# Branch A's normalisation and gate moved into branch B's sample part

## The chip, the cores and the metric

The kernel runs on one core of one Trainium2 chip. The metric is device time in microseconds (us) of one execution of the whole program. Three runs of the kernel before took 2506.22, 2507.71 and 2512.16 us. TensorE is called PE here, VectorE DVE, ScalarE ACT, GpSimd POOL and SyncE SP, as in the profile; ACTq and SPq are the same engines while they issue DMAs.

## The reference

One layer of a decoder is computed for a prompt of 1024 tokens and for 64 sample tokens (8 sequences of 8), 1088 columns in all. Three branches work on one normalised input:

```python
o = ((out - mean) * lax.rsqrt(var + A_GN_EPS)).reshape(B, T, A_WIDTH)   # branch A, after its delta rule
o = o * ln_w.astype(f32) + ln_b.astype(f32)
o = (o + bonus.reshape(B, T, A_WIDTH)) * g                              # g = sigmoid(lg) @ g2
...
x = x + (gates[:, :, 0] * (o_a @ w_branch_a) + gates[:, :, 1] * (o_b @ w_branch_b)
         + gates[:, :, 2] * (o_c @ w_branch_c)) @ w_out
```

Branch A is a recurrent delta rule over 6 heads of width 64, followed by the lines above: mean and variance of each head's 64 outputs, a scale, a bonus and a gate. Branch B is stick-breaking attention over 4 heads: for the prompt over its own 1024 positions, for the samples over 4096 cached positions, which lie in 32 pages of 128 rows for each sequence. Branch C is a dilated window attention. A merge and a feed-forward network follow. The output of branch A is needed only in the merge.

## The kernel before, in words

The stages run one after the other, each a block that all engines enter and leave together: load, projections (`a_project`), the delta rule (`delta`), branch A's normalisation and gate (`a_finish`), branch B's prompt part (`b_prompt`), branch B's sample part (`b_sample`), branch C, merge and feed-forward. Activations lie with channels on the 128 partitions and the 1088 tokens along the row, so branch A's 384 channels are 3 tiles ("pairs" of heads).

`delta` treats the prompt in 16 chunks of 64 tokens (lines 949 to 971) and then the 64 sample tokens (lines 978 to 1068); DVE and ACT copy the new sample states out last (`finish_state`, L779), and SP writes them to memory (L797) and waits for that (L799) before the block can end.

`a_finish` (L1198 to L1328) has the following steps. PE forms the heads' means as products with a block matrix (`put`, L1227, 9 matmuls), DVE subtracts them (L1308), ACT squares (L1278), PE sums the squares with 54 matmuls of two columns (`variance`, L1236), DVE scales (L1312), ACT takes the root (L1291) and DVE the reciprocal (L1315). PE computes the gate product (L1227, 9 more), ACT copies it out (L1283), PE spreads the factors over the partitions with 54 small matmuls (L1250), and DVE applies factor, weight with bonus, and gate (L1320, L1324, L1327). SP loads g2, the bonus and the six tiles of branch B's queries, keys and values (L1219, L1220, L1336).

`b_prompt` (L1356) turns keys and values to rows and then goes through 24 units of a 512-column block against a 128-key block. SP first issues 24 copies of cache windows from memory to memory (L1396, 8 each of 120, 504 and 2040 KB), then four outputs (L1401, L1403), then the first pages of the cache (L1412, L1414).

`b_sample` (L1571) goes through 16 chunks n, each of 4 sequences x 4 pages; it has a software pipeline written out by hand. In loop n, PE turns the keys of chunk n in four parts (`turn`, L1669; DVE copies them out, L1798), scores chunk n-1 (L1680; DVE L1804), turns back the weights of chunk n-2 (L1706; DVE L1849) and multiplies them with the values (L1719). For chunk n-1, ACT computes Abs, Exp and Ln (L1760), DVE makes from them the arguments (`arguments`: L1809, L1813, L1839, L1841), and ACT takes the exponential (L1773). Then ACT issues its share of the page loads of chunk n+2. The 32 pages (keys and values) of a chunk are shared out among the queues of SP (7 pairs), ACT (4) and POOL (5). A ring of 2 holds keys and a ring of 4 holds values: `load(n)` waits until the values of chunk n-4 are used (`pv`) and until part i of chunk n-2 has been turned (`tp`). At the end SP issues branch C's tiles (L1336, 9).

## Time and profile before

| | us |
|---|---|
| median of three runs | 2507.71 |
| the profiled execution | 2505.49 |
| its span in the profile | 2503.8 |
| `delta` ends (last copy by DVE) | at 950.4 |
| `a_finish` | 958.1 to 996.3 |
| `b_prompt` | 997.4 to 1121.5 |
| `b_sample` | 1121.7 to 1325.2 |

The times of the stages are read from the first and the last instruction of each in the timeline. PE is busy for 90% of the span, mostly in the projections and in the feed-forward network, and PEclk is the clock granted to it as a share of full speed.

### The profile page before, as it was taken

What the parts mean: (1) busy time and instruction counts of PE and PEld (TensorE: products, weight loads), DVE (VectorE), ACT (ScalarE), POOL (GpSimd) and SP (SyncE); (2) the same over time, 40 slices, a digit from 0 to 9 for tenths busy, and PEclk for the clock granted to TensorE, in tenths of its full rate; (3) what the DMA queues carried; (4) which work ended last, traced back from release to release, by engine and by line L of the source; (5) the groups of instructions that cost most, each with busy time, mean ns of one, the idle gap of its engine ahead of it and who ended that gap; (6) DMA issues with size and microseconds to landing.
All of it is one profiled execution on the core that took longest, in us unless ns stands there. A gap on an engine that the chain in (4) does not pass through costs nothing. (4 is left out here: it accounts for less than half of the span.)

```text
span 2503.8 us, 45433 instructions
## 1 busy us (share of the span) xinstructions
PE 2263.9 (90%) x19175; PEld 2062.4 (82%) x19175; DVE 1185.4 (47%) x1734; ACT 454.2 (18%) x704; POOL 666.0 (27%) x607
## 2 busy tenths in 40 slices
PE   4999999999989987777778689999999999999986
PEld 3999999999978884434446557999999999999986
DVE  2332322332123323877775444178617735762743
ACT  4000112221011112762224200130000000000012
POOL 3211111112110000554430012434324423332433
PEclk6999999999999997999898899999999999999997
DMA  6112222222210002959996164111111111111113
GB/s 164 47 47 73 79 96 79 94 81 98 86 47 4 4 5 101 323 174 335 348 357 232 63 200 162 51 34 51 34 51 43 46 39 51 43 36 49 43 47 107
DMA packets 252310, 251.92 MB, mean 101 GB/s; under 512 B 22748, under 2 KB 231365, under 8 KB 250428
## 3 DMA queue, kind: packets, MB, share of 16 engines
q1 hardware_dynamic: 213264, 177.32, 22.9%
q10 hardware_dynamic: 31484, 51.60, 6.0%
q0 software_dynamic: 7360, 20.10, 2.4%
q8 instruction: 152, 2.49, 0.4%
q14 instruction: 50, 0.41, 0.1%
HBM read 210.65 MB, written 60.13 MB: 108 GB/s over the span
## 5 line engine op out<-in xcount | busy, mean ns | idle before, releaser
L135 PE MATMUL ps<-ml,fu_wh 128*128 128x352 f32 (+1 forms) x1248 | 408.9, 328 | 7.1 <-POOL fu_wl L129 5.0
L137 PE MATMUL ps<-mh,fu_wl 128*128 128x352 f32 (+1 forms) x1248 | 408.1, 327 | 0.0
L136 PE MATMUL ps<-mh,fu_wh 128*128 128x352 f32 (+1 forms) x1248 | 407.8, 327 | 0.0
L135 PE MATMUL ps<-xl_a,ap_wh 128*128 128x352 f32 (+2 forms) x1200 | 398.4, 332 | 9.1 <-POOL ap_wl L129 9.1
L136 PE MATMUL ps<-xh_a,ap_wh 128*128 128x352 f32 (+2 forms) x1200 | 395.9, 330 | 0.0
L137 PE MATMUL ps<-xh_a,ap_wl 128*128 128x352 f32 (+2 forms) x1200 | 395.2, 329 | 0.0
L697 DVE TENSOR_TENSOR ap_raw<-ps,inv 128x384 f32<-128x384 f32 x150 | 71.2, 531 | 443.4 <-PE ps L137 443.4
L129 POOL TENSOR_TENSOR fu_wl<-fu_wt,fu_wh 128x1024 fp32r<-128x1024 f32 (+2 forms) x92 | 201.4, 2189 | 260.4 <-DVE fu_wh L124 260.4
L129 POOL TENSOR_TENSOR ap_wl<-ap_wt,ap_wh 128x1024 fp32r<-128x1024 f32 x50 | 119.9, 2398 | 513.8 <-DVE ap_wh L124 513.8
L135 PEld LDWEIGHTS ps<-ml,fu_wh 128*128 128x128 f32 x1248 | 234.8, 188 | 8.7 <-POOL fu_wl L129 5.6
L135 PEld LDWEIGHTS ps<-xl_a,ap_wh 128*128 128x128 f32 x1200 | 226.9, 189 | 15.8 <-POOL ap_wl L129 9.6
L136 PEld LDWEIGHTS ps<-mh,fu_wh 128*128 128x128 f32 x1248 | 235.5, 189 | 0.0
L137 PEld LDWEIGHTS ps<-mh,fu_wl 128*128 128x128 f32 x1248 | 234.7, 188 | 0.0
L136 PEld LDWEIGHTS ps<-xh_a,ap_wh 128*128 128x128 f32 x1200 | 226.6, 189 | 0.7 <-issue 0.7
L137 PEld LDWEIGHTS ps<-xh_a,ap_wl 128*128 128x128 f32 x1200 | 226.8, 189 | 0.0
L135 PE MATMUL ps<-fu_al,fu_wh 128*128 128x384 f32 (+1 forms) x528 | 179.3, 340 | 15.3 <-POOL fu_wl L129 10.0
L137 PE MATMUL ps<-fu_ah,fu_wl 128*128 128x384 f32 (+1 forms) x528 | 177.4, 336 | 0.0
L136 PE MATMUL ps<-fu_ah,fu_wh 128*128 128x384 f32 (+1 forms) x528 | 176.9, 335 | 0.0
L2768 DVE TENSOR_TENSOR x<-x,ps 128x352 f32<-128x352 f32 (+2 forms) x117 | 55.9, 528 | 249.5 <-PE ps L137 249.4
L2834 DVE TENSOR_TENSOR o<-ps,inv 128x384 f32<-128x384 f32 x132 | 59.6, 507 | 128.3 <-PE ps L137 128.3
L135 PEld LDWEIGHTS ps<-fu_al,fu_wh 128*128 128x128 f32 x528 | 103.0, 195 | 17.3 <-POOL fu_wl L129 11.5
L1669 PEld LDWEIGHTS ps<-cf,bs_pk 128*128 128x128 f32 x512 | 63.6, 155 | 61.5 <-DMA bs_pk<-in_cache_sb_k 50.9
(451 smaller groups left out, 3510.7 us busy)
## 6 DMA issues: line engine op xcount, KB each, us to landing
ap_wt<-in_w_in SPq DMA_DIRECT2D x50, 512.0 KB, 3.9
fu_wt<-in_w_up SPq DMA_DIRECT2D x44, 512.0 KB, 3.8
scr_pj<-ap_raw ACTq DMA_DIRECT2D x39, 544.0 KB, 2.7
bs_pk<-in_cache_sb_k SPq DMA_DIRECT2D x130, 128.0 KB, 6.7
out_win_sample<-in_cache_win SPq DMA_DIRECT2D x8, 2040.0 KB, 38.1
bs_pv<-in_cache_sb_v SPq DMA_DIRECT2D x121, 128.0 KB, 6.8
mg_gate<-scr_pj SPq DMA_DIRECT2D x24, 544.0 KB, 4.4
bs_pv<-in_cache_sb_v POOLq DMA_DIRECT2D x75, 128.0 KB, 5.8
```

What stands on the lines that cost most here:

```text
L129: return eng.tensor_tensor(dst.bitcast(F32R), x, xh, ALU.subtract)
L135: nc.tensor.matmul(out, wh, xl, start=start, stop=False)
L136: nc.tensor.matmul(out, wh, xh, start=False, stop=False)
L137: return nc.tensor.matmul(out, wl, xh, start=False, stop=stop)
L697: ins = V_.tensor_tensor(raw[:, t % 2, 1 + c0:1 + c0 + n], g.ps[:, 3 * (t % 2) + c, 0:n], g.inv[:, c0:c0 + n], ALU.mult)
L1669: mm = nc.tensor.transpose(g.ps[:, 2 * (i % 2) + p, k * P:(k + 1) * P], pk[:, n % RK, i, k, p * P:(p + 1) * P], g.ident)
L2768: ins = V_.tensor_tensor(x1[:, t, c0:c0 + m], x1[:, t, c0:c0 + m], g.ps[:, 3 * (n % 2) + c, 0:m], ALU.add)
L2834: V_.tensor_tensor(u[:, h, 2 + c0:2 + c0 + m], g.ps[:, b0 + c, 0:m], inv[:, c0:c0 + m], ALU.mult)
```

## The change

- `a_finish` is gone. Its arithmetic is done in `b_sample`, in half-loops ("slots") m = 2(n-1) and 2(n-1)+1 of loop n, in 7 parts of up to 512 columns each: MEAN in slots 0 to 6, VAR in slot 8 (54 matmuls at once), root and reciprocal up to slot 10, SPREAD in 11 to 17, GATE in 18 to 24. Each part is one small group on PE into PSUM bank 7 and one or two instructions on DVE out of it, and the two wait for each other. ACT's three squares stand after the page loads of loops 2, 3 and 4, its root with two table loads after those of loop 5. The gate product is read by DVE straight from PSUM, so ACT's copies of it are gone.
- Bank 7 becomes free because both groups of values now lie in bank 6, in its two halves.
- The sigmoid of the gate's input is computed in `a_project`; the result goes to memory in `delta` (`lgd`) and comes back in `b_prompt` (544 KB each way).
- Branch B's six tiles are loaded in `delta`, the prompt's columns once the prompt's chunks are through (`y`), the samples' columns after `z`. The sample states are written out by SP in `b_prompt`.
- In `b_prompt`, SP issues the small windows, the states, and then each larger window followed by two pages. SP's queue in `b_sample` gets g2 after the loads of n = 2 and the bonus (3 DMAs of 544 KB) after those of n = 8.

The core of the diff:

```diff
@@ delta, SP
+            eng.dma_start(g.lgd, pa[:, AT - 1, :]).then_inc(g.s_lg, 16)
...
-            for b in range(NB):
-                eng.wait_ge(x["fa"], PAIRS)
-                eng.wait_ge(x["fv"], PAIRS)
-                eng.dma_start(g.o["wkv_sample"][0, b].rearrange("h v k -> v h k"), sr[:, b]).then_inc(x["out"], 16)
+            eng.wait_ge(s["y"], 2 * (NU - 1))
+            for i in (2, 3, 4, 5, 0, 1):
+                eng.dma_start(g.qb[:, i, 0:SEQ], g.pj[i][:, 0:SEQ]).then_inc(g.s_qb[i], 16)
+            eng.wait_ge(x["z"], 1)
+            eng.dma_start(g.qb[:, :, SEQ:T], g.pj[0:6].rearrange("a p t -> p a t")[:, :, SEQ:T]).then_inc(g.s_qs, 16)
             eng.wait_ge(s["out"], 16)
-            eng.wait_ge(x["out"], 16 * NB)
+            eng.wait_ge(g.s_lg, 16)
-def a_finish(g):
...
@@ b_prompt, SP
+                for b in range(NB):
+                    window(0, b)
+                for b in range(NB):
+                    eng.dma_start(g.o["wkv_sample"][0, b].rearrange("h v k -> v h k"), g.sr[:, b]).then_inc(g.s_wkv, 16)
...
+                    window(1 + u // NB, u % NB)
+                    page(*pages[2 * u])
+                    page(*pages[2 * u + 1])
+                eng.wait_ge(g.s_wkv, 16 * NB)
+                eng.dma_start(g.oc, g.lgd).then_inc(g.s_lg, 16)
@@ b_sample
+        PARTS = [(None, SEQ, TS)] + [(p, c0, 512) for p in range(PAIRS) for c0 in (0, 512)]
+        NP = len(PARTS)
+        MEAN, VAR, SPREAD, GATE = 0, 8, 11, 11 + NP
+        slot = lambda n, late: 2 * (n - 1) + late
...
+                    if n == 2:
+                        eng.dma_start(g2, a["rwkv_g2"][0]).then_inc(f["w"], 16)
+                    if n == 8:
+                        eng.wait_ge(f["var"], 1)
+                        for p in range(PAIRS):
+                            eng.dma_start(bn[:, p, :], g.bonus[p]).then_inc(f["bn"], 16)
@@ b_sample, PE: branch_a(m), and its place in the loop
+                    elif m == VAR:
+                        eng.wait_ge(f["om"], NP)
+                        eng.wait_ge(f["sq"], PAIRS)
+                        for p in range(PAIRS):
+                            for j in range(NJ):
+                                mm = nc.tensor.matmul(sums[0:rows(j), p, j], sq[:, p, j * P:j * P + rows(j)], g.blk[:, 0:P:HD],
+                                                      start=True, stop=True)
+                        mm.then_inc(f["var"], 1)
...
                     if 1 <= n <= NN:
                         score(n - 1)
+                        branch_a(slot(n, 0))
                     if n < NN:
                         turn(n, 1)
...
                         turn(n, 2)
                         turn(n, 3)
+                    if 1 <= n < NN:
+                        branch_a(slot(n, 1))
@@ b_sample, ACT
                     load(eng, "act", n + RK)
+                    if 2 <= n < 2 + PAIRS:
+                        p = n - 2
+                        eng.wait_ge(f["om"], 2 * p + 3)
+                        nc.scalar.activation(sq[:, p, :], om[:, p, :], ACT.Square).then_inc(f["sq"], 1)
+                    if slot(n, 0) == VAR:
+                        eng.wait_ge(f["ms"], 1)
+                        nc.scalar.activation(nrm[:, :, :, :], nrm[:, :, :, :], ACT.Sqrt).then_inc(f["rt"], 1)
+                        nc.scalar.preload_act_table_set("natural_log_exp_and_others")
@@ b_sample, DVE: an early slot after turned(n, 1), a late one after arguments(n - 1)
+                        V_.tensor_tensor(dst, dst, factor, ALU.mult).then_inc(f["nx"], 1)
+                        if k and c0:
+                            eng.wait_ge(f["nx"], k + 1)
+                            eng.wait_ge(f["bn"], 16 * PAIRS)
+                            V_.scalar_tensor_tensor(out=om[:, p, :], in0=om[:, p, :], scalar=g.col("rwkv_ln_w", p),
+                                                    in1=bn[:, p, :], op0=ALU.mult, op1=ALU.add).then_inc(f["ln"], 1)
```

## Rows read from the trace of the kernel before

**Rows 1.** The page: busy time, share of the span and instructions

```profile
PE 2263.9 (90%) x19175; PEld 2062.4 (82%) x19175; DVE 1185.4 (47%) x1734; ACT 454.2 (18%) x704; POOL 666.0 (27%) x607
```

**Rows 2.** Busy time by stretch: us, engines, PEclk, DMA share, GB/s

```profile
950.50:997.40 46.90, 29.94 (x198) 21.89 (x198) 17.27 (x28) 9.54 (x15) 0.00 (x0) 0.75 0.37 128
997.40:1121.70 124.30, 95.73 (x420) 50.45 (x420) 103.50 (x137) 84.76 (x102) 65.08 (x50) 0.93 0.78 246
1144.10:1299.90 155.80, 119.13 (x1098) 75.32 (x1094) 113.45 (x136) 32.79 (x52) 65.00 (x122) 0.92 1.08 348
1179.50:1187.50 8.00, 7.30 (x79) 4.78 (x72) 5.94 (x7) 1.93 (x4) 4.42 (x9) 1.00 1.09 349
```

**Rows 3.** Timeline from delta's end to b_prompt: start, us, engine, line, work

```profile
918.70 0.64 SPq L792 DMA_DIRECT2D out_wkv_prompt<-dp_so  x1
...
949.76 0.68 DVE L779 COPY o<-ps 64x512 f32<-64x512 f32 x1 [0.19 <-PE ps L1066]
950.53 5.45 SPq L797 DMA_DIRECT2D out_wkv_sample<-o  x8
...
994.97 1.35 DVE L1327 SCALAR_TENSOR_TENSOR o<-om,par,af_gate 128x1088 f32<-128x1088 f32 x1
997.40 0.33 SPq L1389 DMA_DIRECT2D bq_later<-c_later  x1
...
1015.57 51.65 SPq L1403 DMA_DIRECT2D out_sb_k_sample<-pa  x1
```

**Rows 4.** DMA: moved in 40 slices of 1122:1325 and 1293:1318; an issue

```profile
GB/s 175 304 268 319 353 344 352 345 347 349 346 350 350 346 348 347 349 350 349 346 345 348 352 347 346 345 347 347 348 352 347 346 348 352 344 374 411 366 37 0
...
GB/s 334 359 354 352 336 341 364 346 334 356 341 338 355 359 381 381 401 415 383 415 418 390 418 425 425 383 430 397 383 418 425 411 348 306 209 139 97 42 21 0
...
pa<-scr_pj SPq DMA_DIRECT2D x6, 544.0 KB, 9.5
```

**Rows 5.** SP's waits in b_sample: total us, times, longest

```profile
SPq L1623 <- PE ps L1719: 3.2, 5, 0.9
```

**Rows 6.** Timeline of b_sample's loop 5, and two groups over 1144.1:1299.9

```profile
1179.41 0.15 DVE L1841 TENSOR_TENSOR bs_later<-bs_later,bs_l 128x1 f32<-128x1 f32 x1
1180.33 0.34 ACTq L1626 DMA_DIRECT2D bs_pk<-in_cache_sb_k  x1
1180.57 1.09 PE L1669 MATMUL ps<-cf,bs_pk 128*128 128x128 f32 x8
1184.77 1.93 PE L1719 MATMUL ps<-bs_pv,pa 128*32 128x256 f32 x32
1186.14 0.63 ACT L1760 ACTIVATE bs_l<-bs_x 128x512 f32<-128x512 f32 x1 [5.92 <-issue]
1188.13 0.69 DVE L1809 SCALAR_TENSOR_TENSOR bs_l<-bs_x,bs_l 128x512 f32<-128x512 f32 x1 [1.63 <-ACT bs_l L1760]
1189.94 0.34 SPq L1626 DMA_DIRECT2D bs_pk<-in_cache_sb_k  x1
...
L1798 DVE COPY bs_kT<-ps 128x1024 f32<-128x1024 f32 x52 | 62.9, 1220 | 31.3 <-PE ps L1680 15.6 <-PE ps L1669 15.4
L1839 DVE SCALAR_TENSOR_TENSOR bs_x<-bs_x,bs_later,bs_l 128x512 f32<-128x512 f32 x14 | 10.5, 752 | 0.5
```

**Rows 7.** Groups of instructions in a_finish: busy us, mean ns, idle before

```profile
L1227 PE MATMUL ps<-o,aux 128*128 128x352 f32 (+1 forms) x18 | 8.5, 644 | 8.5 <-PEq L782 8.5
L1236 PE MATMUL ps<-aux,af_sq 128*128 128x2 f32 (+1 forms) x54 | 6.5, 249 | 0.0
L1308 DVE SCALAR_TENSOR_TENSOR om<-ps,o 128x352 f32<-128x352 f32 (+1 forms) x9 | 4.3, 529 | 5.6 <-PE ps L1227 5.6
L1320 DVE TENSOR_TENSOR om<-om,ps 128x512 f32<-128x512 f32 (+1 forms) x9 | 4.2, 526 | 8.0 <-PE ps L1250 8.0
L1278 ACT ACTIVATE af_sq<-om 128x1088 f32<-128x1088 f32 x3 | 3.3, 1110 | 6.6 <-DVE om L1308 6.6
L1291 ACT ACT_TABLE_LOAD x1 | 1.3, 1283 | 0.0
```

More of the change, by code:

```diff
@@ L1580, in b_sample, with before @@
     NN = NG * NC
+    NJ = SEQ // P + 1
+    rows = lambda j: P if j < NJ - 1 else TS
+    PARTS = [(None, SEQ, TS)] + [(p, c0, 512) for p in range(PAIRS) for c0 in (0, 512)]
+    NP = len(PARTS)
+    MEAN, VAR, SPREAD, GATE = 0, 8, 11, 11 + NP
+    slot = lambda n, late: 2 * (n - 1) + late
+    done = lambda m, first: max(0, min(m - first, NP))
+    def before(m):
+        return done(m, MEAN), done(m, SPREAD), done(m, GATE)
     with ExitStack() as ctx:
         sb = lambda name, shape, dt=F32: ctx.enter_context(nc.sbuf_tensor(f"bs_{name}", shape, dt))
+        oa = g.oa
+        om, sq, bn = g.pa[:, 4:7, :], g.pa[:, 1:4, :], g.pa[:, 1:4, :]
+        g2 = g.pa[:, 7, 0:AW]
+        nrm = g.pa[:, 8, 0:PAIRS * NJ * 2].rearrange("t (p j h) -> t p j h", j=NJ, h=2)
+        sums = g.ps[:, 7, 0:PAIRS * NJ * 2].rearrange("t (p j h) -> t p j h", j=NJ, h=2)
         pk, pv1 = g.pk, sb("pv1", [P, RV - 1, GB, UP, 256])
@@ L1682, in score, with branch_a @@
                     mm.then_inc(s["z"], 1)
+                def branch_a(m):
+                    mean, bc, gate = before(m)
+                    if MEAN <= m < MEAN + NP:
+                        if m == MEAN:
+                            eng.wait_ge(s["zn"], 1)
+                        eng.wait_ge(f["om"], mean)
+                        put(m - MEAN, lambda p: g.blk, oa, "mean")
+                    elif m == VAR:
[6 more added lines that the diff above has]
+                        mm.then_inc(f["var"], 1)
+                    elif SPREAD <= m < SPREAD + NP:
+                        eng.wait_ge(f["rv"], 1)
+                        eng.wait_ge(f["nx"], bc)
+                        p, c0, n = PARTS[m - SPREAD]
+                        for q in range(PAIRS) if p is None else (p,):
+                            for j in (NJ - 1,) if p is None else range(c0 // P, c0 // P + 4):
+                                at = q * TS if p is None else j * P - c0
+                                for h in range(2):
+                                    mm = nc.tensor.matmul(g.ps[HD * h:HD * h + HD, 7, at:at + rows(j)],
+                                                          nrm[0:rows(j), q, j, h:h + 1].broadcast_to([rows(j), HD]),
+                                                          g.ident[0:rows(j), 0:rows(j)], start=True, stop=True)
+                        mm.then_inc(f["bc"], 1)
+                    elif GATE <= m < GATE + NP:
+                        eng.wait_ge(f["nx"], NP)
+                        eng.wait_ge(f["oa"], gate)
+                        if m == GATE:
+                            eng.wait_ge(f["w"], 16)
+                            eng.wait_ge(g.s_lg, 32)
+                        put(m - GATE, lambda p: g2[:, p * P:(p + 1) * P], None, "g")
@@ L1684, in turn_new, with put @@
+                def put(k, lhs, rhs, inc):
+                    p, c0, n = PARTS[k]
+                    for q in range(PAIRS) if p is None else (p,):
+                        at = q * TS if p is None else 0
+                        src = g.oc[:, c0:c0 + n] if rhs is None else rhs[:, q, c0:c0 + n]
+                        mm = nc.tensor.matmul(g.ps[:, 7, at:at + n], lhs(q), src, start=True, stop=True)
+                    mm.then_inc(f[inc], 1)
                 def turn_new():
```

227 lines of the change are left out of this document (80 added, 147 removed).

## The prediction

> **What bounds the kernel now.** The page's busy times come first: PE is busy for 90% of the span [rows 1], but the stages touched here are not of that kind, so they are read alone, from the table by stretch [rows 2]. Three things are to be seen in it.
>
> The 46.9 us between the last work of `delta` and the first of `b_prompt` hold only 29.94 us of PE and 17.27 us of DVE, at a clock of 0.75: a chain of short steps between engines, with nothing beside it.
>
> `b_prompt` takes 124.3 us with DVE busy for 103.5 us and the DMA engines for a share of 0.78. DVE bounds it, and the DMAs have a fifth of the time left.
>
> `b_sample` is bound by its page loads. Over 13 whole loops, from the first to the last of 14 starts of L1839 [rows 6], 155.8 us, the DMA share is over 1 at 348 GB/s, and the rate by slices is flat at 344 to 353 GB/s from the fifth slice to the 35th [rows 2, 4]. That is 155.8/13 = 11.98 us a loop. The engines have room inside it: per loop PE is busy 9.2 us and DVE 8.7 us. But a second cycle is nearly as long. From the end of DVE's arguments (1179.56) ACT takes the exponential, issues its four page pairs until 1186.1 and computes Abs, Exp and Ln until 1188.1; DVE then needs 0.69 (L1809), some 1.2 (the scan) and 0.75 (L1839) until 1190.8 [rows 6]. That is some 11.2 us. So compute can catch up some 0.8 us a loop on the DMAs, no more.
>
> **The change, part by part.**
>
> 1. The stage goes. Before, DVE's last copy ends at 949.76 + 0.68 = 950.44, SP then issues the states until 955.98 and waits for them, `a_finish` starts at 958.1, its last instruction ends at 996.32, and SP's first issue of `b_prompt` is at 997.40, 1.08 us later [rows 3]. After the change nothing is left to be waited for at the end of `delta`, so `b_prompt` starts 1.08 us after 950.44, at 951.5. Saved: 997.40 - 951.5 = 45.9 us.
>
> 2. The six tiles must be there by then. SP is free after the prompt's state went out at 918.7 [rows 3] and can issue the six about then. Before, such a tile landed 9.5 us after its issue, with 3 us to issue six [rows 4], so the last lands near 932. The samples' columns follow `z`, near 931, in 256-byte pieces: between 3 us and the whole 9.5 us of a tile, of which I take 4, so 935. Cover: 16 us. Without it the late part would stand on the path one for one. Cost 0.
>
> 3. `lgd` out of `delta` and the sigmoid in `a_project` lie beside idle engines. In `b_prompt` the DMAs get the same copies plus the states (0.8 MB) and `lgd` (0.56 MB), 1.4 MB or 4 us at 348 GB/s, into 124.3 x 0.22 = 27 us of room [rows 2]. SP's issues are now held up behind the copies in another order. Before, the queue held one output's issue for 51.65 us [rows 3] and the stage did not suffer. Bounds 0 and +15; I take 0.
>
> 4. Bytes in `b_sample`: g2 and bonus, 0.2 + 1.67 = 1.87 MB in a stage where DMA is the bound. At the page loads' 348 GB/s that is 5.4 us; at 411 GB/s, which the slices show when the tiles of branch C come in [rows 4], 4.5 us. I take 5. The four issues themselves cost SP under 2 us, and SP is not behind otherwise. The Trainium skill, page "DMA: Bandwidth & Descriptors", section "Where 436 GB/s comes from", sets about 358 GB/s as the limit of one core on the memory side. By that the bytes cost 5.2 us. The flat 348 agrees, the 381 to 425 GB/s of the tiles go beyond it, so the trace decides.
>
> 5. The MEAN slots (loops 1 to 4), and likewise GATE (10 to 13). A 512-column part costs PE 0.64 us x 512/362 = 0.9 and DVE 0.53 x 512/362 = 0.75 [rows 7]. Two of them a loop make DVE's 8.7 us 10.2 and PE's 9.2 us 11, both under 11.98. What counts is the time while ACT is busy from 1179.56 to 1188.1: 8.5 us. DVE worked 5.94 us in that stretch [rows 2], and with the two parts 7.4. It fits. The waits between PE and DVE in bank 7 may add between 0 and 1 us a loop; there are eight such loops, and I take 0 for them, since the ends of the slots fall in the gaps. Upper bound +8.
>
> 6. ACT's squares cost 1.11 us each [rows 7], right behind the page issues and ahead of Abs. ACT is in the second cycle, so loops 2 and 3 get 1.1 us longer: +2.2, before the DMAs are the bound. I count them in compute's path.
>
> 7. VAR, loop 5. This is the dear step. PE has it behind the scoring of chunk 4, where the turn of part 1 stood before, at 1180.57 [rows 6]. It waits there for the third square. But ACT does that one after its page issues, when before it began Abs, at 1186.14; so it ends at 1187.3. PE stands still for 6.7 us, and queued behind it are the turns of parts 1 to 3, the turn back and the values of chunk 3. Then come 54 matmuls, 6.5 us [rows 7], until 1193.8; the turn of part 1, 1.09; DVE's copy of it 1.22, its own VAR part 0.4, the copy of the turn back 0.7, two copies of turns 2.4 [rows 6], so L1809 starts at about 1199.6 where it started at 1188.13: +11.5 us in compute's path. The values of chunk 3, which started at 1184.77, end at about 1199.3 and not at 1186.7. All three queues wait for them before the loads of chunk 7 (a ring of 4). SP started these at 1189.94 [rows 6] and was held by such waits for only 3.2 us in the whole stage [rows 5]. Now it starts at 1199.4. All that was issued before is 11 half-chunks of 2.1 MB from 1122.5 on, 23 MB, which at the slices' rates is drained at about 1191.5. So the DMA engines stand idle for 1199.4 - 1191.5 = 8 us.
>
> 8. The root with two table loads: a root over 54 columns, under 0.3, and 2 x 1.28, together 2.8 us of ACT behind the issues of loop 5 [rows 7], in compute's path. The Trainium skill ("ScalarE: Activation LUTs", "Table sets: the hidden batching unit") prices exp followed by sqrt at two loads, some 5.3 us; by that the step would be 5.5 us. The row has 1.283 us for a load, half of the page's, and is used.
>
> 9. SPREAD, loops 7 to 9: two factors and a whole weight-and-bonus pass, 2 x 0.65 (L1320, 0.526 us for 363 columns, at 512 with the fixed part) + 1.35 (as long as L1327) = 2.7 us of DVE a loop [rows 3, 7], so 8.6 us in the 8.5 us of ACT's cover. At most 0.5 us each, 1.5 in all, in compute's path.
>
> **The sum.** Two paths run beside each other. Compute: 2.2 + 11.5 + 2.8 + 1.5 = 18, of which the eight loops after the stall give back 0.8 us each, 6.4, and the lead that the DMAs left before it, some 3: about +9. DMA: 8 idle + 5 bytes = +13. The longer one ends the stage: `b_sample` +13. Net 45.9 - 13 = 32.9 us less. The profiled execution took 2505.5 us and would take 2472.6. The median shown is 2.2 us above that execution, so the forecast is 2475 us. Its own range, with step 7 between 9 and 17 and step 5 between 0 and 4, is 2470 to 2482.
>
> **The rivals.**
>
> A. The stall is absorbed. The DMA share hardly falls at loop 5, because 7 us of landing time are in flight, and only the bytes cost: +5, so 2507.7 - 45.9 + 5 = 2467. For it: the loads are issued up to two chunks ahead. Against it: the order of issues in rows 6, where SP's loads of chunk 7 stand only 3 us behind the values that release them.
>
> B. DVE and PE become the bound in all the loops with slots. The added DVE work, 4.3 + 4.2 + 4.1 + 4.1 us and 1 us of small ones, 17.7 us in all, comes in full on top of the stall, the squares and the root, 16.5: +34, or 2496. For it: DVE and PE wait for each other twice a loop. Against it: 27% of DVE's and 24% of PE's time in this stretch is idle.
>
> C. Slower than before. Every slot of bank 7 is a meeting of PE and DVE, and each engine works off its list strictly in order. There are 22 slots. If a slot made PE wait for DVE's late part, behind the scan, and DVE for PE's, the price would be PE's 0.9, DVE's 0.75 and half of the scan and argument work, 1.5: some 3.1 us each, 68 us, and with it 2530. It decides from 45.9/22 = 2.1 us a slot. Against it: the loop's own waits are already of this kind, and much of them is slack.
>
> D. `b_prompt` is held by SP's new order. The last copies of 2040 KB are issued near its end, SP leaves the block late by some 10 us, and the sum is 2485.
>
> E. The change doesn't do what it says: the tiles land only after 951.5 because they are issued late. A full reload costs some 12 us: 2487.
>
> **How the numbers follow.** Forecast 0.45, A 0.2, B 0.2, C 0.04, D 0.06, E 0.02, the rest (a gain elsewhere) 0.03. The range takes the forecast's, A's and most of the way to B: 2463 to 2491. A measurement of this kernel can tell 0.3% from no change, 7.5 us. Only C and the far end of B or D come near that: faster 0.94, the same 0.02, slower 0.04.
>
> **What would show it.** `b_prompt` starts at 951 to 952, takes 124 us, and its first transposes don't wait for tiles. In `b_sample` PE has one gap of about 7 us ahead of a run of 54 two-column matmuls, and SP, ACT and POOL all pause their page issues there; the GB/s by slices has one hole and is flat on both sides. The stage takes 216 us. ACT has two table loads in loop 5 and none at the squares. The forecast is wrong if there is no hole (then A), if the rate is below 340 GB/s in the MEAN, SPREAD and GATE loops too (then B), or if the block before ends late by its DMAs (D).

## The result

The kernel after the change takes 2499.23 us in the median of six runs (2494.34 to 2501.34), the kernel before 2506.92 us on the same chip (2506.22 to 2512.16). The ratio is 0.9952, with a 95% interval of 0.9937 to 0.9966: 7.7 us faster by the medians, where 32.9 us were forecast. The profiled executions span 2497.9 us and, before, 2503.8 us.

The page's first rows for the kernel after answer to [rows 1]: the engines' total work is the same, as it should be, and the total says nothing about where the 46 us of the removed stage went.

```profile
span 2497.9 us, 45428 instructions
PE 2263.7 (91%) x19175; PEld 2063.4 (83%) x19175; DVE 1183.3 (47%) x1736; ACT 451.8 (18%) x696; POOL 665.7 (27%) x607
```

So the stages are timed one by one, each from the first instruction of its block to that of the next, read from the timelines (`b_prompt` from SP's load of `bq_later`, `b_sample` from POOL's clearing of `bs_qz`, branch C from SP's load of `cq_jbias`, the merge from its first matmul).

| | before | after |
|---|---|---|
| `b_prompt` starts at | 997.40 | 952.28 |
| `b_prompt` lasts | 124.4 | 126.0 |
| `b_sample` lasts | 203.5 | 238.3 |
| branch C lasts | 124.9 | 125.5 |

45.1 us are gained up to the start of `b_prompt`, 1.6 us are lost in it, and 34.8 us in `b_sample`, where 13 were forecast. Branch C and what follows it took 2.7 us more in this profile, with nothing changed in them, so that the spans differ by 5.9 us. The first gain shows in the timeline of the kernel after (start, us, engine, line, work): SP issues the six tiles at 920.24, `delta`'s last copy ends at 951.27, and `b_prompt` starts 1.01 us later. PE's first transposes then wait for the block's entry, not for a tile.

```profile
920.24 3.52 SPq L800 DMA_DIRECT2D pa<-scr_pj  x6
...
932.24 0.37 SPq L802 DMA_DIRECT2D pa<-scr_pj  x1
...
950.59 0.68 DVE L782 COPY o<-ps 64x512 f32<-64x512 f32 x1 [0.19 <-PE ps L1071]
952.28 0.33 SPq L1259 DMA_DIRECT2D bq_later<-c_later  x1
...
952.62 1.07 PE L1309 MATMUL ps<-cf,pa 128*128 128x128 f32 x8 [2.06 <-PEq L155]
```

The busy times of the two stages (columns as in [rows 2]) answer to its second row. `b_prompt` is as it was. `b_sample`'s DMA share is down to 0.87 over the stage, so the loads are no longer what fills it:

```profile
952.30:1078.00 125.70, 97.12 (x420) 50.91 (x420) 103.28 (x137) 84.72 (x102) 65.20 (x50) 0.92 0.77 254
1078.00:1316.60 238.60, 180.28 (x1596) 117.63 (x1596) 161.55 (x219) 48.67 (x75) 78.33 (x147) 0.88 0.87 285
```

The rate in 40 slices of 1078 to 1310 us, 5.8 us each, shows where. Before it was flat from the fifth slice on [rows 4]. Now there are three holes: slices 13 to 16 (1148 to 1171), slices 23 to 25 (1206 to 1223) and slices 29 and 30 (1240 to 1252); slices 18 and 19 (1177 to 1188) are a shallower dip.

```profile
GB/s 166 304 275 353 350 348 255 330 349 353 347 347 253 0 3 187 325 255 267 354 378 365 329 13 244 339 347 348 184 282 358 349 347 350 346 350 346 379 409 254
```

The lengths of the chunk loops, from one start of DVE's arguments (L1839 before, L1809 after) to the next, say the same from the compute side:

```
before  11.3 11.1 12.3 11.4 12.3 11.6 12.7 11.5 13.9 11.0 11.4 13.3 12.1 10.2
after   11.9 12.6 12.1 28.8 14.5 11.9 24.2 11.5 17.6 11.3 11.4 11.1 12.3 11.3
```

**The first long loop (28.8 us)** holds VAR. In the timeline ACT takes the third square behind its page issues, PE waits 8.55 us for it, and then the 54 matmuls take 11.46 us where [rows 7] had 6.5. DVE's copy of the next turn comes after 19.11 us of waiting, and SP, which issued its last page at 1147.78, gets to the next one at 1165.68.

```profile
1144.16 1.11 ACT L1740 ACTIVATE pa<-pa 128x1088 f32<-128x1088 f32 x1 [5.60 <-issue]
...
1145.41 11.46 PE L1611 MATMUL ps<-aux,pa 128*128 128x2 f32 x54 [8.55 <-ACT pa L1740]
...
1147.78 0.34 SPq L1534 DMA_DIRECT2D bs_pv<-in_cache_sb_v  x1
1158.81 1.23 DVE L1768 COPY bs_kT<-ps 128x1024 f32<-128x1024 f32 x1 [19.11 <-PE ps L1583]
...
1165.68 0.35 SPq L1533 DMA_DIRECT2D bs_pk<-in_cache_sb_k  x1
...
1173.54 1.28 ACT L1743 ACT_TABLE_LOAD   x1 [6.21 <-issue]
1174.84 0.25 ACT L1743 ACTIVATE pa<-pa 128x54 f32<-128x54 f32 x1
1175.10 1.28 ACT L1744 ACT_TABLE_LOAD   x1
```

Three stretches of that loop, before, in and behind the run of 54: PE is idle in the first, busy for the whole of the second at a granted clock of 0.50, that is, 1.2 GHz, and is not back at full clock in the third.

```profile
1137.80:1145.40 7.60, 0.00 (x0) 0.02 (x1) 1.90 (x4) 1.87 (x3) 2.88 (x6) 0.76 1.08 350
1145.40:1156.90 11.50, 11.49 (x55) 11.40 (x56) 0.00 (x0) 1.65 (x3) 0.00 (x0) 0.50 0.61 193
1156.90:1165.70 8.80, 8.80 (x72) 7.52 (x76) 6.30 (x9) 0.00 (x0) 0.00 (x0) 0.70 0.01 2
```

**The second (24.2 us)** is something that the prediction did not have at all. SP issues the bonus behind the pages of chunk 8 at 1191.56, and DVE's first pass with it is due 2 us later, in slot 13. It waits 13.15 us; DVE's copies of the next keys stand behind it, and so do PE's next turns and all page loads. From the first of the three issues until the wait ends the DMAs are not idle: they move 366 GB/s, 5.6 MB, of which the bonus is 1.67 MB and the rest pages issued earlier (the last row, columns as in [rows 2]).

```profile
1191.56 1.37 SPq L1547 DMA_DIRECT2D pa<-scr_bn  x3
...
1192.97 0.68 DVE L1858 TENSOR_TENSOR pa<-pa,ps 128x512 f32<-128x512 f32 x1
1206.80 1.35 DVE L1862 SCALAR_TENSOR_TENSOR pa<-pa,par 128x1088 f32<-128x1088 f32 x1 [13.15 <-DMA pa<-scr_bn]
...
1191.56:1206.80 15.24, 3.87 (x44) 2.30 (x32) 2.06 (x4) 0.63 (x1) 5.01 (x10) 0.77 1.06 366
```

**The third (17.6 us, 13.9 before)** is the loop with the first group's output. PE waits 4.67 us for DVE's copy of it, ahead of which DVE has 2 us of slot work:

```profile
1228.70 0.68 DVE L1858 TENSOR_TENSOR pa<-pa,ps 128x512 f32<-128x512 f32 x1
1229.41 1.35 DVE L1862 SCALAR_TENSOR_TENSOR pa<-pa,par 128x1088 f32<-128x1088 f32 x1
1230.68 0.41 DVE L1823 COPY bs_o<-ps 128x256 f32<-128x256 f32 x1
1231.15 0.69 PE L1686 MATMUL ps<-cf,bs_o 128*128 128x128 f32 x2 [4.67 <-DVE bs_o L1823]
```

Behind that wait PE does its next work, the turn of the output, a turn of keys and the scoring, in 5.90 us at a granted clock of 0.50; before, the same work took 4.73 us at 0.64, behind a wait of 3.61 us. So the wait costs its own length and then slower matmuls. First the row before, then after:

```profile
1239.34:1244.07 4.73, 4.73 (x26) 1.83 (x26) 0.76 (x4) 0.27 (x1) 2.93 (x6) 0.64 1.09 350
```

```profile
1231.15:1237.05 5.90, 5.90 (x27) 2.59 (x27) 0.76 (x4) 0.00 (x0) 3.12 (x6) 0.50 1.08 348
```

SP's waits for the values (total us, times, longest) sum it up. [rows 5] had 3.2 us; now it is

```profile
SPq L1530 <- PE ps L1678: 35.7, 5, 16.4
```

### The profile page after: what moved, and what is told of

It reads as the page before. It is cut to its first block and busy times, and to the rows that moved or that the text cites. A ratio compares the mean times of both kernels' runs of the same rounds, so it can differ in the third digit from the quotient of the medians.

```text
span 2497.9 us, 45428 instructions
## 1 busy us (share of the span) xinstructions
PE 2263.7 (91%) x19175; PEld 2063.4 (83%) x19175; DVE 1183.3 (47%) x1736; ACT 451.8 (18%) x696; POOL 665.7 (27%) x607
## 5 line engine op out<-in xcount | busy, mean ns | idle before, releaser
L135 PEld LDWEIGHTS ps<-xl_a,ap_wh 128*128 128x128 f32 x1200 | 226.9, 189 | 15.9 <-POOL ap_wl L129 9.7
L2862 DVE SCALAR_TENSOR_TENSOR o<-o,cw 128x1104 f32<-128x1104 f32 x44 | 109.9, 2498 | 1.6
```

The lines of the kernel that those rows point to most:

```text
L135: nc.tensor.matmul(out, wh, xl, start=start, stop=False)
L2862: V_.scalar_tensor_tensor(out=cv[:, h, 0:E], in0=u[:, h, 1:1 + E], scalar=column(g.cw[:, 1], h, j), in1=cv[:, h, 0:E], op0=ALU.mult, op1=A ...
```

## The experiments

All are variants of the changed kernel. Each was timed in five rounds beside the kernel before; the ratio is to the latter. Stage lengths and matmul times are those of each one's one profile. "The sums" are the 54 matmuls of VAR. The stage length of one profile and the median of its kernel need not agree to better than 2 or 3 us.

| | median us (range) | ratio, interval | `b_sample` | PE idle ahead of the sums | the 54 sums |
|---|---|---|---|---|---|
| the change again | 2496.97 (2494.23–2499.98) | 0.9945 [0.9932, 0.9959] | 237.2 | 8.61 | 11.47 |
| bonus early | 2486.78 (2482.14–2488.36) | 0.9903 [0.9888, 0.9917] | 226.0 | 8.34 | 11.46 |
| squares first | 2487.29 (2486.61–2488.77) | 0.9909 [0.9893, 0.9924] | 227.7 | 0.89 | 7.73 |
| both | 2479.52 (2476.07–2480.96) | 0.9871 [0.9856, 0.9886] | 218.2 | 2.62 | 10.68 |
| both, once more | 2479.91 (2474.64–2486.59) | 0.9876 [0.9857, 0.9895] | 220.4 | 2.58 | 11.24 |
| both, output first | 2476.13 (2472.56–2481.49) | 0.9870 [0.9852, 0.9889] | 213.6 | 1.17 | 8.08 |
| no arithmetic in slots | 2475.97 (2472.31–2480.32) | 0.9871 [0.9849, 0.9893] | 215.3 | | |
| also no bonus and g2 | 2471.37 (2468.22–2475.05) | 0.9845 [0.9826, 0.9865] | 207.7 | | |
| both, sums a slot later | 2481.57 (2478.25–2487.34) | 0.9890 [0.9871, 0.9909] | 219.9 | 0 | 11.33 |
| the same, 16 columns | 2483.46 (2477.58–2487.58) | 0.9886 [0.9862, 0.9909] | 220.6 | 0 | 11.47 |
| change, sums a slot later | 2488.50 (2485.04–2493.53) | 0.9920 [0.9902, 0.9938] | 227.8 | 1.42 | 11.46 |
| the same, in three slots | 2479.29 (2477.09–2481.70) | 0.9873 [0.9855, 0.9892] | 219.8 | 2.51 (third) | 2.05, 2.15, 3.85 |
| both, three slots | 2479.06 (2477.56–2483.93) | 0.9880 [0.9858, 0.9902] | 213.7 | 0 | 2.05, 2.15, 2.05 |
| and bonus by pair | 2476.96 (2470.14–2481.17) | 0.9866 [0.9844, 0.9889] | 212.9 | 0 | 2.05, 2.15, 2.05 |
| and 16 columns | 2478.19 (2472.82–2478.84) | 0.9873 [0.9852, 0.9895] | 210.8 | 0 | 2.08, 2.18, 2.08 |
| by pair, output first | 2476.75 (2473.41–2478.48) | 0.9861 [0.9842, 0.9881] | 213.7 | 0 | 2.05, 2.15, 2.05 |

**The change again.** The same kernel, on the chip of the next three, as their base.

> The changed kernel as it is, for comparison on the same chip with the next three. Both theories: 2499 us, 7 to 8 below before.

**Bonus early.** The three loads two chunks earlier in SP's list:

```diff
-                    if n == 8:
+                    if n == 6:
                         eng.wait_ge(f["var"], 1)
```

> SP issues the three bonus loads after the page loads of chunk 6 in place of chunk 8, where the trace after has SP waiting some 16 us for the values of chunk 3. Theory 1 (the gain was lost at two places, the wait for the bonus, 13.2 us, and the stall around the 54 sums of squares, 17 us): the 13.2 us of DVE's wait for scr_bn vanish, loop 7 goes from 24 us back to some 13, and the time falls by 9 to 12 us against the changed kernel, to about 2489. Theory 2 (the slots' meetings of PE and DVE cost a little in every loop, and the DMAs bound the rest): the wait is hidden by the page loads anyway, and less than 3 us comes back.

10.2 us less than the change on the same chip, and `b_sample` 11.2 less. The first hole and its 28.8 us loop stay as they were; the loop of 24.2 us is 12.0. The group row of the three passes, then that of the changed kernel (busy us, mean ns, idle ahead): the wait is gone, nothing else about the passes has changed.

```profile
L1862 DVE SCALAR_TENSOR_TENSOR pa<-pa,par 128x1088 f32<-128x1088 f32 x3 | 4.1, 1352 | 0.1
```

```profile
L1862 DVE SCALAR_TENSOR_TENSOR pa<-pa,par 128x1088 f32<-128x1088 f32 x3 | 4.1, 1351 | 13.2 <-DMA pa<-scr_bn 13.2
```

But the edit also moves the bytes. The three loads are now issued at 1156.84, in the first hole, where the DMAs stand otherwise idle, and land 3.3 to 5.6 us after their issues, for 8.1 to 14.2 before. In that stretch the DMAs move 247 GB/s, 1.69 MB, which is just the bonus:

```profile
1156.84:1163.70 6.86, 6.86 (x52) 6.26 (x56) 4.44 (x7) 0.00 (x0) 0.00 (x0) 0.62 0.70 247
```

So the 11.2 us hold two things that this run doesn't separate: the wait, and up to 4.8 us (1.67 MB at 348 GB/s) for bytes that no longer stand in the way of pages.

**Squares first.** ACT squares ahead of its page issues:

```diff
-                    load(eng, "act", n + RK)
                     if 2 <= n < 2 + PAIRS:
                         ...
+                    load(eng, "act", n + RK)
```

> ACT does each square ahead of its four page pairs, not behind them. Theory 1: PE's idle time before the sums falls from 8.6 us to about 2 to 3 us; and since the clock granted to PE was 0.5 in the 54 matmuls after that idle time, they should take 6.5 us again, not 11.5, so the loop falls from 28.8 us to some 17 and the time by 8 to 11 us against the changed kernel. If the clock has nothing to do with the idle time ahead, the matmuls stay at 11.5 us and only 5 to 6 us come back. Theory 2: 0 to 3 us.

9.7 us less. The idle time ahead of the sums falls from 8.6 to 0.89 us, and the sums need 7.73 us, not 6.5; the loop falls from 28.8 to 18.7 us. Three stretches, the second and third being the sums: the clock is 1.00 before them and in their first 4 us, and 0.56 in the rest, though PE is busy throughout.

```profile
1129.49:1137.49 8.00, 6.27 (x68) 3.20 (x66) 6.12 (x8) 2.77 (x5) 2.79 (x6) 1.00 1.09 348
...
1138.38:1142.38 4.00, 4.00 (x35) 3.95 (x36) 1.14 (x2) 0.00 (x0) 2.65 (x5) 1.00 1.08 351
1142.38:1146.11 3.73, 3.73 (x22) 3.68 (x22) 0.00 (x0) 1.89 (x3) 0.00 (x0) 0.56 1.07 346
```

**Both.**

> Both moves together. Theory 1: the two gains add up nearly fully, 16 to 22 us against the changed kernel, about 2480, and the branch B sample part takes some 218 us. Theory 2: under 5 us.

17.5 us less than the change, close to the sum of the two, 19.9: the two waits are, nearly, separate losses. `b_sample` is 218.2 us. These are near the numbers forecast for the change (216 us, 2475), but of another kernel, with a shorter wait ahead of the sums (2.62 us) than the 6.7 us of the forecast.

**No arithmetic in the slots, and then no loads either.** The first leaves out every instruction of branch A in `b_sample` on PE, DVE and ACT and keeps its loads; the second leaves out the loads too.

```diff
-                    if n == 2:
-                        eng.dma_start(g2, a["rwkv_g2"][0]).then_inc(f["w"], 16)
-                    if n == 8:
-                        for p in range(PAIRS):
-                            eng.dma_start(bn[:, p, :], g.bonus[p]).then_inc(f["bn"], 16)
```

> The changed kernel without any of branch A's arithmetic in the slots (no mean, no sums, no root, no spread, no gate on PE, DVE and ACT); all its loads stay. It gives the price of all slots together. Theory 1 as it now stands (stage before: 45 us saved; bytes some 5; the rest of the loss is in the slots, and of it the two stalls are 20): the branch B sample part takes 203.5 + 5 = 209 us, and the whole 2469. If the extra bytes are free too: 2464. If the lost time were not in the slots but in what else moved (the order of the loads, the bank that both value groups share), it would stay at 2480 or above.

> The kernel without any of branch A's arithmetic in b_sample's slots, and now also without the bonus's three loads and the gate weights' load (so branch A is neither normalised nor gated, and 1.87 MB are not read). With the loads but without the arithmetic the stage b_sample took 215.3 us against 203.5 before, its chunk loop 8 took 20.8 us with TensorE waiting 9.7 us for key pages, and the kernel 2475.97. Theory 1: those 12 us are the loads in SP's queue, between pages that the next loops need; without them b_sample takes 203 to 206 us, no loop is over 14 us, and the kernel 2464 (2461 to 2468). Theory 2: they come from the stage's place (it starts earlier against the prefetches and evictions of branch B's prompt part, or its page loads stand in another order); then b_sample stays at 212 to 216 and the time at 2473 to 2477.

The first was a miss. With no arithmetic at all the stage is still 11.8 us longer than before; its longest loop, of 20.8 us, comes behind the bonus, where PE waits for keys:

```profile
1191.06 1.97 PE L1584 MATMUL ps<-cf,bs_pk 128*128 128x128 f32 x8 [9.68 <-DMA bs_pk<-in_cache_sb_k]
```

Without the loads 7.6 of the 11.8 us are gone, and no loop exceeds 15.7 us. The kernel is 4.6 us faster by the medians and 6.5 by the ratios, whose intervals overlap. So the loads, where they stand, cost some 5 to 8 us with no arithmetic beside them; the 5 us of the forecast are not refuted. The second expectation missed too, in both its theories (2471.37 us, for 2464 or 2473 and more). The last 4.2 us against the kernel before come with the stage's new place or the profile's own spread, and stay open.

**Sums a slot later.** `VAR` from slot 8 to 9, `SPREAD` and `GATE` one further; once in the version with both edits and once in the change alone.

```diff
-    MEAN, VAR, SPREAD, GATE = 0, 8, 11, 11 + NP
+    MEAN, VAR, SPREAD, GATE = 0, 9, 12, 12 + NP
```

> Both earlier moves, and the sums of squares one slot later, behind the four turns of loop 5 instead of ahead of three of them; spread and gate one slot later as well. Theory 1: the 54 matmuls no longer stand ahead of the turns that DVE waits for, so the loop of 21.8 us becomes some 15 to 17 and the time falls by another 4 to 7 us against the kernel with both moves, to about 2474. Rival (PE's own work is what the loop is short of, wherever it stands): under 2 us.

> The changed kernel with nothing but the sums one slot later (bonus and squares as changed). It tells how much of the stall is the wait for the third square and how much the order on PE. Theory 1: by the time of the late slot the square is done, PE does not stand still before the sums and stays at full clock, so it gains as much as moving the squares did, 8 to 12 us against the changed kernel, about 2487, with the bonus wait unchanged at 12 to 13 us. Rival (the 54 matmuls alone are the price): no more than 3 us.

Theory 1 missed in both. The first gained nothing, as its rival had it: the loop with the sums takes 25.3 us where 15 to 17 were expected, and the kernel 2481.57 us, for 2479.52 without this move (the intervals overlap). No wait stands right ahead of the sums, and they take 11.33 us all the same. In the 8 us before them PE was busy for only 4.38 us, and the clock had fallen before they began (mean 0.84):

```profile
1137.20:1145.20 8.00, 4.38 (x29) 3.92 (x29) 4.83 (x5) 2.46 (x4) 2.91 (x6) 0.84 1.08 348
1145.20:1156.53 11.33, 11.33 (x59) 11.23 (x62) 3.93 (x6) 0.63 (x1) 0.00 (x0) 0.50 0.55 175
```

The other expected full clock and had 0.50 (11.46 us). It did gain on the change, 8.5 us by the medians and 6.3 by the ratios, but with shorter waits: 1.42 us ahead of the sums for 8.55, and 6.76 us for the bonus for 13.15.

**Sums in three slots.** One pair's 18 matmuls in each of slots 7, 8 and 9:

```diff
-                    elif m == VAR:
+                    elif VAR - 2 <= m <= VAR:
+                        p = m - VAR + 2
                         eng.wait_ge(f["om"], NP)
-                        eng.wait_ge(f["sq"], PAIRS)
-                        for p in range(PAIRS):
-                            for j in range(NJ):
+                        eng.wait_ge(f["sq"], p + 1)
+                        for j in range(NJ):
```

> As the last one, and the 54 sums in three slots of 18 (one pair of heads each, slots 7, 8 and 9). Theory 1: no piece is longer than 2 to 4 us, the loops 4 and 5 take 12 to 14 us each, and it comes within 5 us of the kernel without slots, about 2472. Rival: three more meetings of PE and ACT cost what the split gains, same as the last one within 2 us.

> The changed kernel with the sums of squares in three slots of 18 matmuls (one pair each, the last one slot later than before), squares and bonus as they are in the change. With the 54 in one piece in the same slot: 2488.50 us, the 54 in 11.46 us, the stage 227.8. Theory 1: a long unbroken run of them is what lets TensorE's clock fall; in three pieces they take 6 to 7 us in all, the stage is 3 to 6 us shorter and the kernel 2484 (2481 to 2487). Theory 2: the clock falls for the waiting ahead of them, and is as low in the pieces; then 11 us in all and 2487 to 2490.

With both edits the pieces run at full clock and take 6.3 us in all, which is about [rows 7]'s price. The stage is 213.7 us, 4.5 less than with both edits alone, but the median is the same (2479.06 for 2479.52); in that profile branch C, which no edit touches, took 129.3 us for 125.1. The clock did not stay up, though: it fell right behind the first and the third piece, with PE busy throughout.

```profile
1130.52:1132.57 2.05, 2.05 (x24) 2.02 (x26) 2.05 (x3) 0.71 (x2) 0.45 (x1) 1.00 1.09 349
1132.90:1136.20 3.30, 3.30 (x34) 1.52 (x23) 2.31 (x3) 0.85 (x2) 0.00 (x0) 0.50 1.06 340
```

In the change alone, with late squares and late bonus, splitting brings 9.2 us against the unsplit version (2488.50; by the ratios 0.47%, 11.8 us), more than theory 1 expected, and 2479.29 us is what the two moves together reach. The sums themselves are 3.4 us shorter; the rest comes with the loop around them, which falls from 25.0 to 16.9 us. Its three pieces: the first two at full clock, the third behind a wait of 2.51 us at half.

```profile
1131.96 2.05 PE L1611 MATMUL ps<-aux,pa 128*128 128x2 f32 x18
...
1138.68 2.15 PE L1611 MATMUL ps<-aux,pa 128*128 128x2 f32 x18
...
1146.84 3.85 PE L1611 MATMUL ps<-aux,pa 128*128 128x2 f32 x18 [2.51 <-ACT pa L1740]
```

So both theories of that pair hold a part. The clock was at half behind a wait, and with the squares first it fell inside the unbroken run. The kernel before shows the second by itself: PE is busy for all of 10.20 us, the last 3.5 of them in a run of 36 such matmuls, and then gets half the clock for 6.3 us without having been idle.

```profile
963.70:973.90 10.20, 10.20 (x66) 8.38 (x64) 2.84 (x6) 5.74 (x7) 0.00 (x0) 1.00 0.89 359
973.90:980.20 6.30, 6.30 (x15) 4.03 (x15) 0.76 (x3) 1.44 (x4) 0.00 (x0) 0.50 0.00 0
```

**More columns.** The same 54 matmuls with 16 columns, every eighth sum read:

```diff
-sums[0:rows(j), p, j], sq[:, p, j * P:j * P + rows(j)], g.blk[:, 0:P:HD]
+wsum[0:rows(j), p, j], sq[:, p, j * P:j * P + rows(j)], g.blk[:, 0:P:8]
```

> The version with the bonus early, the squares ahead of the page loads and everything from the sums on one slot later (2481.57 us; its 54 matmuls of two columns took 11.33 us with no idle time ahead of them, clock 0.51), and the 54 matmuls now have 16 columns each (the same block matrix at every eighth column, of which VectorE reads every eighth sum). Theory 1: the clock falls because two-column matmuls leave TensorE's array idle most of the time; with 16 columns it does not fall or falls later, the 54 take 6.5 to 8 us and the kernel 2478 to 2480. Theory 2: the clock falls for what went before (the wait of the loop, or plain fp32 weight loads, which are as many in both); then the 54 take 11 to 12 us again and the time stays within 2 us of 2481.6.

11.47 us at 0.50, as with two columns (11.33): that the matmuls are narrow is not what lets the clock fall, at least not between 2 and 16 columns.

**Bonus by pair**, each load behind the pages of n = 6, 7 and 8 with a semaphore of its own; and the same with 16 columns:

```diff
-                    if n == 6:
-                        eng.wait_ge(f["var"], PAIRS)
-                        for p in range(PAIRS):
-                            eng.dma_start(bn[:, p, :], g.bonus[p]).then_inc(f["bn"], 16)
+                    if 6 <= n < 6 + PAIRS:
+                        eng.wait_ge(f["var"], n - 5)
+                        eng.dma_start(bn[:, n - 6, :], g.bonus[n - 6]).then_inc(f[f"bn{n - 6}"], 16)
```

> The version with squares ahead of the page loads and their sums in three slots (2479.06 us, b_sample 213.7), with the bonus loaded one pair at a time, after the pages of n = 6, 7 and 8, and VectorE waiting for each pair by itself. Theory 1: it is the burst of 1.6 MB in a queue that is served in order that makes key pages late by 7.9 us (loops of 15.2 and 15.9 us in that version); three pieces of 0.53 MB each cost 1.5 us at 350 GB/s and fit between pages; b_sample 207 to 210, the kernel 2474 (2471 to 2477). Theory 2: bytes are bytes, whatever their order: 1.57 MB at 350 GB/s is 4.5 us of a stage that DMA bounds at 0.87 busy; then b_sample stays within 2 us of 213.7 and the kernel within 2 us of 2479.

> The version with the bonus spread by pair and, on top of it, matmuls of 16 columns for the sums (three slots of 18). In pieces of 18 the two-column sums already took 2.1 us a piece, so by theory 1 (the clock falls only in a long run of them) the wider columns bring nothing: within 1.5 us of the spread version, 2474. By theory 2 (each short run still lowers the clock of the matmuls behind it) some 2 us are gained, 2472.

PE's longest wait for keys falls from 5.33 to 3.19 us, and the three loops of 15.2, 15.9 and 12.7 us (43.8) become 14.4, 13.2 and 14.2 (41.8). The stage is 0.8 us shorter and the medians differ by 2.1 us with intervals that overlap: no gain from the order is shown, once nobody waits for these loads. With 16 columns on top it is 2478.19 us, 1.2 more, within the scatter, and the pieces take 2.08, 2.18 and 2.08 us, as theory 1 had it. In both versions the clock stays at 1.00 through the loops with the sums, so the fall behind a piece of 18 does not come each time.

**Output first.** In DVE's list, the copy of a group's output ahead of branch A's late slot:

```diff
-                    if 1 <= n < NN:
-                        branch_a(slot(n, 1))
                     if n >= 2 and chunk(n - 2) == 0:
                         out(group(n - 2))
+                    if 1 <= n < NN:
+                        branch_a(slot(n, 1))
```

> The version with the sums in three slots and the bonus spread by pair (2476.96 us), where VectorE now copies the first group's output ahead of branch A's work of that slot, and not behind it. In the changed kernel TensorE stood idle for 4.67 us in that loop (17.6 us against 13.9 before) because VectorE did 2.03 us of slot work (L1858, L1862) ahead of that copy. Theory 1: that slot work stands in the path; the loop, 16.7 us in the spread version, falls to 14 to 15 us, the stage by 1 to 2.5 us, the kernel to 2475 (2473 to 2477). Theory 2: the loads bound this loop too; the loop gets shorter, others longer, and the stage stays at 212.9 +- 1.

Nothing moved in the time: the loop is 16.1 us for 16.6, the stage 213.7 for 212.9, the time the same. But the run tested little. With everything one slot later, the slot that meets the output (17) holds only the factor L1858, 0.68 us, and PE's wait went from 3.98 to 3.38 us, that is, by this much. The expectation had priced it by the changed kernel's slot, 2.03 us. So the same exchange was made where the slot is as in the changed kernel, beside its twin.

> The version with the bonus early and the squares ahead of the page loads (2479.52 us), where VectorE copies a group's output ahead of branch A's work of that slot. Here, as in the changed kernel, that slot work is 2.03 us (L1858 and L1862) and TensorE waits 5.28 us for the copy; in the version tried before, everything came a slot later and only 0.68 us stood ahead of the copy, so that edit tested little. Theory 1: the slot work stands in the path of the loop with the output (16.4 us, 13.9 before the change); TensorE's wait falls by 2 us to some 3.3, the loop to some 14.5, and the kernel gains 1 to 2.5 us on its twin of this call. Theory 2: the loads bind across these loops and what the loop gains its neighbours lose; TensorE's wait falls all the same, and the time is within 1 us of its twin.

> The version with the bonus early and the squares ahead of the page loads once more, as the twin on the same chip: 2477 to 2482 us and b_sample at 218 us by either theory; TensorE's wait for the first group's output is 5.3 us and the loop with it 16.4 us.

The loop with the output takes 12.9 us in the one and 17.4 in the twin, and the third hole is gone. PE's wait was not what was expected: 2.75 us, and 3.46 in the twin. Of the 4.5 us between the loops, 2.03 are the slot work. Nearly all the rest is the clock behind the wait: the turn of the output, a turn of keys and the scoring take 3.1 us at 1.00 with the output first, and 5.7 us at 0.53 in the twin.

```profile
1204.90:1208.00 3.10, 3.07 (x26) 1.49 (x26) 2.44 (x6) 0.30 (x1) 2.13 (x4) 1.00 1.12 356
```

```profile
1213.40:1219.10 5.70, 5.68 (x27) 2.60 (x27) 0.75 (x4) 0.00 (x0) 3.74 (x7) 0.53 1.08 348
```

The slices of 1080 to 1310 us, first with the output first, then the twin (whose hole is at slices 26 and 27):

```profile
GB/s 287 272 313 352 350 288 305 356 349 346 351 346 381 330 345 211 317 359 349 348 348 348 348 347 350 348 347 347 349 347 350 347 369 412 327 2 0 331 407 408
```

```profile
GB/s 147 294 287 348 347 349 344 353 347 347 350 346 335 214 283 354 155 306 359 350 347 348 347 350 345 151 281 359 346 347 349 348 351 347 384 409 218 0 122 357
```

The slot work ahead of the copy, with the lower clock that followed the longer wait, is what made that loop long, as far as one profile of each can show. A price in the kernel's time is not shown: the medians differ by 3.8 us, but the ratios by 0.0006 only (1.5 us), well within their intervals. The profiled executions are the fastest of the one (2472.56 us) and the slowest of the other (2486.59), and they also differ in the sums (8.08 and 11.24 us), which the edit doesn't touch.

## Why the prediction was wrong

The sign, the 45.9 us of the removed stage (45.1 measured) and the place and shape of the first loss were right; the loss in `b_sample` was 34.8 us and not 13. Two steps failed: step 4 priced the bonus as bytes and not as a wait, and step 7 had the run of 54 matmuls at 6.5 us where it took 11.46. Point by point:

1 and 2. The stage goes, and the tiles are there: right within 1 us. `b_prompt` started at 952.28 for 951.5 forecast.

3. SP's new order in `b_prompt`: right within its bounds. It cost 1.6 us, against 0 taken.

4. "Bytes in `b_sample`", 5 us, "and SP is not behind otherwise". The 5 us for the bytes stand (4.6 to 7.6 us when the loads were left out), but the step priced the bonus only as bytes, not as something that a DVE instruction waits for. The order of issues would have shown it. The loads of chunk 8 wait for the values of chunk 4; the bonus stands behind them, so it could not be issued before loop 7, and the first pass is due in loop 7. It shared the DMAs with the pages that were already issued, so it was all there only 15 us after its first issue (1191.56 to 1206.80), where 1.67 MB at 348 GB/s are 4.8 us. The Trainium skill ("DMA: Bandwidth & Descriptors", "Queues, rings and completion order") says that each DMA engine takes the descriptors of one ring in their order; these 15 us agree with that, though the trace can't tell the order in SP's queue from the share that the other two queues took. The prediction did not reckon with any such delay. The missed term is 13.15 us of wait. The early bonus, which took it away, gave back 10.2 us of the kernel's time and 11.2 us of the stage, part of it for the bytes that moved into the first hole.

5, 6 and 8. MEAN and GATE slots, squares, root: about right, but for one place. "The ends of the slots fall in the gaps" did not hold in the loop with the first group's output, where a slot stands in DVE's list ahead of the copy that PE waits for (17.6 us, 3.7 more than before; 12.9 with the two exchanged). The loops with them but without a wait are 11.1 to 12.6 us; no table load came with the squares, and the root with its two loads of 1.28 us took 2.84 us, for 2.8 forecast.

7. The stall was there, as forecast, in PE's list behind the late third square (8.55 us for 6.7). "Then come 54 matmuls, 6.5 us [rows 7]" is the mis-sized term: 11.46 us. The row was a group over two runs of the kernel before, 18 and 36 matmuls at 114 and 124 ns each, with wide matmuls of the gate between them, as its timeline shows:

```profile
966.48 2.05 PE L1236 MATMUL ps<-aux,af_sq 128*128 128x2 f32 x18
968.46 2.10 PE L1227 MATMUL ps<-pa,g 128*128 128x384 f32 x6
970.39 4.45 PE L1236 MATMUL ps<-aux,af_sq 128*128 128x2 f32 x36
```

In the new place they are one run of 54 behind a wait, at half the clock (212 ns each). The earlier row held the sign of this: the clock fell there too, 3.5 us into the run of 36. The loop with it grew by 17.4 us instead of 11.5, and the next ones by 2.2 us more.

9. SPREAD: the arithmetic fits as forecast (loops of 12.0 and 11.4 us with the bonus early). The first of its loops is where the missed wait stands.

The sum. The forecast was 8 us of idle DMAs and 5 us of bytes. The stretches of the three holes and of the dip between the first two, in the kernel after:

```profile
1147.60:1170.80 23.20, 22.43 (x150) 19.22 (x150) 10.26 (x14) 0.63 (x1) 3.21 (x6) 0.68 0.36 111
1205.60:1223.00 17.40, 13.47 (x129) 9.86 (x130) 16.03 (x19) 2.52 (x4) 3.47 (x7) 0.78 0.62 195
1240.40:1252.00 11.60, 11.35 (x98) 6.99 (x98) 11.26 (x17) 1.33 (x3) 4.27 (x8) 1.00 0.74 233
1176.60:1188.20 11.60, 11.50 (x120) 7.32 (x116) 10.19 (x14) 2.31 (x4) 4.84 (x10) 0.88 0.85 261
```

Against 348 GB/s they are worth 15.8, 7.6, 3.8 and 2.9 us of transfer, 30.2 in all (an estimate from these rates; other slices lie a little above or below 348). With 5.4 us for 1.87 MB at the same rate that makes 35.6 us, against 34.8 measured. So the stall that was forecast at 8 us was worth 15.8, and the rest was not in the forecast: the wait for the bonus, the loop with the output, and the dip, which no run takes apart (the root and its table loads stand just ahead of it).

Of the rivals, A (the stall absorbed) is refuted by the hole in the slices; B's time, 2496, is near the result, but not its mechanism: with both waits taken out and all the DVE and PE work left in, the kernel takes 2479.52 us, 3.6 us more than the one without any of that work, at the same ratio (0.9871). That pair has the bonus at different places, but the best full version gives the same answer against the kernel with neither that work nor its loads: 212.9 us of stage for 207.7, and 2476.96 us for 2471.37, where B has 34 us. C, D and E did not occur.

The best full versions here are the change with the squares and the bonus early and the output first (2476.13 us, 0.9870 [0.9852, 0.9889]), and with the sums in three slots and the bonus by pair, without and with the output first (2476.96 us, 0.9866 [0.9844, 0.9889], and 2476.75 us, 0.9861 [0.9842, 0.9881]). They are 1.3 to 1.4% faster than the kernel before and some 20 us faster than the change, and cannot be told apart. That this is near the 2475 us forecast for the change is chance: these are other kernels, and the change itself missed.

## What to carry to other kernels

When work moves into another stage's slots, follow each of its loads as a wait, not only as bytes: which load it is queued behind, what gates that one, and which instruction is due when. When an instruction group's price is taken from a grouped row, look at how the group was broken up there; one long run of small matmuls behind a wait had another clock than the same matmuls in pieces. A wait can also cost more than its length, when the clock falls in it and the matmuls behind it are slower. An engine that works off its list in order turns either mistake into a stop of all page loads, and these stops nearly added up here: 10.2 and 9.7 us alone, 17.5 together.

## What was not expected of the hardware

- PE can be busy without a break and still be granted 1.2 GHz: 0.50 over 11.33 us of 54 small fp32 matmuls with no idle time right ahead, and a fall from 1.00 to 0.56 inside such a run. Pieces of 18 between other work ran at full clock themselves, 2.05 us, but in one version the clock fell to 0.50 for some 3 us right behind two of the three, and in two others it didn't; a piece behind 2.51 us of waiting took 3.85 us. Whether the columns are 2 or 16 made no difference (11.33 and 11.47 us). The Trainium skill ("TensorE: Matmul & The Clock Gate", "What's actually happening") says that the clock is set by how busy PE has been of late. The half clock behind PE's idle stretch agrees (0.76, then 0.50). A run that is busy for 11.33 of 11.33 us and stays at 0.50 does not, nor does the kernel before, where PE is busy for 10.20 of 10.20 us and then gets 0.50, if busy is what the profile counts as busy, and here the measurement decides. What exactly the clock follows is not settled by these runs.
- The same three loads of 544 KB landed 8.1 to 14.2 us after their issues beside page loads, and 3.3 to 5.6 us after them when issued into a stretch in which the page loads had stopped. When a load is issued set its landing more than its size.
